# Differential score matmuls: the key's low part taken as 64-row products of both maps, and tiles of queries regrouped

## The reference

```python
p1 = causal_block_probs(q[:, start:end, :, 0], k[:, :end, :, 0], start, scale)
p2 = causal_block_probs(q[:, start:end, :, 1], k[:, :end, :, 1], start, scale)
p = (p1 - lam * p2).astype(v.dtype)
outs.append(jnp.einsum('bhqk,bkhd->bqhd', p, v[:, :end]))
```

## Time and profile before

| | |
|---|---|
| median of 3 runs | 1959.62 us |
| the profiled execution's own time | 1960.08 us |
| its span, first to last instruction | 1958.3 us |
| granted TensorE clock, mean over the span | 0.999 of full |
| TensorE matmuls: busy, count | 1946.1 us (99%), 9316 |
| TensorE weight loads: busy | 1630.9 us (83%) |
| DVE, ACT, POOL busy | 53%, 47%, 54% |
| one head of stage B, from one head's first score matmul to the next's | 38.12 us |

### The profile page before, as it was taken

One profiled execution on the slowest core, in us unless ns is written; L12 is line 12 of the kernel. 1 busy time (PEld: TensorE's weight loads), 2 busy tenths in 40 slices (PEclk: granted clock), 3 DMA queues, 4 the chain that ended last, 5 costly groups with the idle time before them and its releaser, 6 DMA issues.

```text
span 1958.3 us, 28641 instructions
## 1 busy us (share of the span) xinstructions
PE 1946.1 (99%) x9316; PEld 1630.9 (83%) x9316; DVE 1035.7 (53%) x1906; ACT 928.1 (47%) x1648; POOL 1066.7 (54%) x1418
## 2 busy tenths in 40 slices
PE   9999999999999999999999999999999999999998
PEld 7888888888888888888888888888888888888887
DVE  5555888887655333321154668888875543333111
ACT  6344666676544222233344456666674442222332
POOL 5655454444555555557765645345445555555674
PEclk9999999999999999999999999999999999999999
DMA  6332222224542322233343322222245332222232
GB/s 248 109 120 86 87 85 88 76 81 138 191 145 86 107 96 96 96 110 96 104 135 121 114 81 92 81 79 90 90 161 185 117 101 94 99 96 95 82 93 91
DMA packets 117938, 212.62 MB, mean 109 GB/s; under 512 B 14290, under 2 KB 31698, under 8 KB 117332
## 3 DMA queue, kind: packets, MB, share of 16 engines
q1 hardware_dynamic: 100944, 176.47, 27.3%
q10 hardware_dynamic: 16900, 34.92, 5.0%
HBM read 194.03 MB, written 17.31 MB: 108 GB/s over the span
## 4 chain that ended last, share of the span: by engine, by line
PE 99%; DMA 0%; DVE 0%; ACT 0%; issue 0%; SPq 0%
PE proj L599 24%; PE proj L601 24%; PE proj L600 24%; PE score L599 2%; PE score L600 2%; PE score L601 2%; PE flip L672 2%; PE score L654 2%; PE score L832 1%; PE score L834 1%; PE score L658 1%; PE score L657 1%; PE att L580 1%; PE att L581 1%; PE att L579 1%; PE score L846 1%
## 5 line engine op out<-in xcount | busy, mean ns | idle before, releaser
L556 POOL TENSOR_TENSOR w_lo<-raw,w_hi 128x256 fp32r<-128x256 f32 x1372 | 1061.6, 806 | 870.2 <-ACT w_hi L1126 870.0
L599 PE MATMUL proj<-h_hi,w_hi 128*128 128x512 f32 x1568 | 619.2, 395 | 0.0
L601 PE MATMUL proj<-h_hi,w_lo 128*128 128x512 f32 x1568 | 611.7, 390 | 0.0
L600 PE MATMUL proj<-h_lo,w_hi 128*128 128x512 f32 x1568 | 610.7, 389 | 0.0
L1126 ACT ACTIVATE w_hi<-raw 128x1024 fp32r<-128x1024 f32 x344 | 362.7, 1056 | 193.7 <-PE proj L601 55.5
L601 PEld LDWEIGHTS proj<-h_hi,w_lo 128*128 128x128 f32 x1568 | 294.3, 188 | 62.6
L599 PEld LDWEIGHTS proj<-h_hi,w_hi 128*128 128x128 f32 x1568 | 294.6, 188 | 58.4 <-issue 0.6
L600 PEld LDWEIGHTS proj<-h_lo,w_hi 128*128 128x128 f32 x1568 | 294.8, 188 | 58.2
L599 PE MATMUL proj<-hid_hi,w_hi 128*128 128x512 f32 x330 | 129.0, 391 | 0.0
L601 PE MATMUL proj<-hid_hi,w_lo 128*128 128x512 f32 x330 | 128.5, 389 | 0.0
L600 PE MATMUL proj<-hid_lo,w_hi 128*128 128x512 f32 x330 | 128.4, 389 | 0.0
(11 more groups left out here) (408 smaller groups left out, 3146.2 us busy)
## 6 DMA issues: line engine op xcount, KB each, us to landing
raw<-in_w_in SPq DMA_DIRECT2D x224, 256.0 KB, 2.8
raw<-in_w_gate_up SPq DMA_DIRECT2D x176, 256.0 KB, 2.8
raw<-in_w_down SPq DMA_DIRECT2D x96, 192.0 KB, 2.4
gate_in<-gate_scratch ACTq DMA_DIRECT2D x48, 256.0 KB, 4.2
gate_scratch<-gate_out ACTq DMA_DIRECT2D x46, 256.0 KB, 2.0
raw<-in_w_mem_kv SPq DMA_DIRECT2D x32, 256.0 KB, 2.8
raw<-in_w_o_diff SPq DMA_DIRECT2D x32, 256.0 KB, 2.8
raw<-in_w_out SPq DMA_DIRECT2D x32, 256.0 KB, 2.8
```

What stands on the lines that cost most here:

```text
L556: ins = g.tensor_tensor(w_lo[s][:, cols], raw[s % 2][:, cols], w_hi[s][:, cols].bitcast(F32), ALU.subtract)
L599: mm(o, hi[:, c:c + width], rh, start=start and k == 0, stop=False)
L600: mm(o, hi[:, c:c + width], rl, start=False, stop=False)
L601: ins = mm(o, lo[:, c:c + width], rh, start=False, stop=stop and k == n - 1)
```

## The change

- The key's low parts of both maps lie in one tile `k_lo`: map 1's in rows 0 to 63, map 2's in rows 64 to 127. The zero halves and the two memsets that wrote them are gone.
- The low matmuls take 64 rows instead of 128: map 1's rows 0 to 63 of the array, map 2's rows 64 to 127. They stand alternately in the program and write different banks. One pair would share a bank; there TensorE waits on a semaphore of its own (`lower_done`).
- A step no longer holds one map but both maps of half the query tiles: first the long step (t = 3 and t = 1, 512 and 256 columns), then the short step (t = 2 and t = 0, 384 and 128 columns). In each the four high matmuls come first and then the four low ones. Maxima, exponentials, inverse sums, scaling and the combination follow this grouping; the second map's long tiles go to a new buffer `p_c`, and map 1's scaling is in two parts, of which the second stands behind a weight split on ACT.
- The short step waits for 6 of the head's 12 exponentials instead of 8.
- The latent scores keep a function of their own without the branch for maps. `SPLIT` swaps outputs 10 and 6, since `p_c` lies over part of `outs_hi`, and ACT's wait for `att_read` in the last head stands earlier. In `last_head` the calls change as in `head`. Semaphore counts follow (`score_full` 8 a head instead of 9, `inv_ready` and `p_scaled` 2 instead of 1).

```diff
-SPLIT = (0, 1, 2, 3, 4, 5, 8, 9, 10, 6, 12, 13, 11, 14, 15, 7)
+SPLIT = (0, 1, 2, 3, 4, 5, 8, 9, 6, 10, 12, 13, 11, 14, 15, 7)
...
-        k1_lo, k2_lo = over_x("k1_lo_zero", 4), over_x("k2_zero_lo", 5)
+        k_lo = over_x("k1_lo_k2_lo", 4)
...
-                for k in ("m", "d1", "d2")}
-        lam_scale = here("lam_scale", [P, NT])
+                for k in ("m", "long", "short")}
+        lam_scale = {k: here(f"lam_scale_{k}", [P, NT]) for k in ("long", "short")}
...
+        p_c = at("p_c", 53 * KB, [P, 6 * P])
...
+        def map_tiles(part):
+
+            if part == "long":
+                return ((score[0][:, 0:512], 0, 3), (score[1][:, 0:512], 1, 3), (score[2][:, 0:256], 0, 1), (score[2][:, 256:512], 1, 1))
+            return ((score[0][:, 0:384], 0, 2), (score[0][:, 384:512], 0, 0), (score[1][:, 0:384], 1, 2), (score[1][:, 384:512], 1, 0))
+
+        def map_home(part, second, t):
+
+            if not second:
+                return p_b[:, q_off(t):q_off(t) + (t + 1) * P]
+            if part == "short":
+                return p_a[:, q_off(t):q_off(t) + (t + 1) * P]
+            return p_c[:, 0:512] if t == 3 else p_c[:, 512:768]
...
-            def causal_scores(l, h, n):
-
-
-                pe.wait_ge(exp_done.sem, exp_done.at(l, "B", h, 4 * n))
+            def map_scores(l, h, part):
+
+                pe.wait_ge(exp_done.sem, exp_done.at(l, "B", h, 4 if part == "long" else 6))
+                upper, lower = slice(0, 64), slice(64, P)
+                for n, (o, second, t) in enumerate(map_tiles(part)):
+                    q, k = ((q1, k1), (q2, k2))[second]
+                    opens = n != 3 if part == "long" else n % 2 == 0
+                    mm(o, q[:, t * P:(t + 1) * P], k[:, 0:(t + 1) * P], start=opens, stop=False)
+
+                def low(b, c, second, t, k0, width, stop):
+                    rows, q = (lower, q2) if second else (upper, q1)
+                    return mm(score[b][:, c:c + width], q[rows, t * P:(t + 1) * P], k_lo[rows, k0:k0 + width], start=False, stop=stop)
+                if part == "long":
+                    low(2, 256, 1, 1, 0, 256, False).then_inc(lower_done.sem, 1)
+                    low(0, 0, 0, 3, 0, 512, True).then_inc(score_full.sem, 1)
+                    low(1, 0, 1, 3, 0, 512, True).then_inc(score_full.sem, 1)
+                    pe.wait_ge(lower_done.sem, lower_done.at(l, "B", h, 1))
+                    low(2, 0, 0, 1, 0, 256, True).then_inc(score_full.sem, 1)
+                else:
+                    for t, c, last in ((2, 0, False), (0, 384, True)):
+                        for second in range(2):
+                            ins = low(second, c, second, t, 0, (t + 1) * P, last)
+                            if last:
+                                ins.then_inc(score_full.sem, 1)
+
+            def causal_scores(l, h):
+
+                pe.wait_ge(exp_done.sem, exp_done.at(l, "B", h))
                 for b, group in enumerate(((3,), (2, 0), (1,))):
                     for t in group:
                         o = score[b][:, 384 * (t == 0):384 * (t == 0) + (t + 1) * P]
                         cols = slice(t * P, (t + 1) * P)
-                        if n == 0:
-                            ins = mm(o, mqT[0:96, cols], mkT[0:96, 0:(t + 1) * P], start=t != 0, stop=t == group[-1])
-                        else:
-                            q, k, k_lo = ((q1, k1, k1_lo), (q2, k2, k2_lo))[n - 1]
-                            mm(o, q[:, cols], k[:, 0:(t + 1) * P], start=t != 0, stop=False)
-                            ins = mm(o, q[:, cols], k_lo[:, 0:(t + 1) * P], start=False, stop=t == group[-1])
+                        ins = mm(o, mqT[0:96, cols], mkT[0:96, 0:(t + 1) * P], start=t != 0, stop=t == group[-1])
                     ins.then_inc(score_full.sem, 1)
...
-                causal_scores(l, h, 1)
+                map_scores(l, h, "long")
                 causal_flip(l, h, 0, 0)
                 unit(l, "B", h, 1, 1, (ssq_read, ssq_read.at(l, "B", h)) if h else (v_copied, v_copied.at(l, "B", 0, 1)),
                      KD, h_rhs, w=w(1)).then_inc(slot_done.sem, 1)
                 causal_flip(l, h, 0, 1)
-                causal_scores(l, h, 2)
+                map_scores(l, h, "short")
                 unit(l, "B", h, 2, 0, (v_copied, v_copied.at(l, "B", n, 1)), KD, h_rhs, w=w(2)).then_inc(slot_done.sem, 1)
                 latent_attend(l, h)
...
+            def map_exps(l, h, part):
+
+                _, bias, total, _ = stat[part]
+                act.wait_ge(bias_ready.sem, bias_ready.at(l, "B", h, 2 if part == "long" else 3))
+                for c, (src, second, t) in enumerate(map_tiles(part)):
+                    sc.activation(map_home(part, second, t), src, ACT.Exp, bias=bias[:, c:c + 1], scale=DIFF_SCALE,
+                                  accum_out=total[:, c:c + 1]).then_inc(exp_done.sem, 1)
...
-            def scale_first(l, h):
-
-                act.wait_ge(inv_ready.sem, inv_ready.at(l, "B", h, 1))
-                for t in range(NT):
-                    s = p_b[:, q_off(t):q_off(t) + (t + 1) * P]
-                    ins = sc.activation(s, s, ACT.Copy, scale=stat["d1"][3][:, t:t + 1])
+            def scale_first(l, h, part):
+
+                act.wait_ge(inv_ready.sem, inv_ready.at(l, "B", h, 1 if part == "long" else 2))
+                for c, (_, second, t) in enumerate(map_tiles(part)):
+                    if not second:
+                        s = map_home(part, 0, t)
+                        ins = sc.activation(s, s, ACT.Copy, scale=stat[part][3][:, c:c + 1])
                 ins.then_inc(p_scaled.sem, 1)
...
-                exps(l, "B", h, 1, "d1", p_b, DIFF_SCALE)
+                map_exps(l, h, "long")
                 split_ahead(l, "B", h, 1, h)
                 causal_high(l, h, 0, 1)
-                scale_first(l, h)
+                scale_first(l, h, "long")
                 if h:
                     act.wait_ge(att_read.sem, att_read.at(l, "B", h))
                     outs_high(l, h - 1)
                 act.wait_ge(flip_full.sem, flip_full.at(l, "B", h, 4))
-                exps(l, "B", h, 2, "d2", p_a, DIFF_SCALE)
+                map_exps(l, h, "short")
                 split_ahead(l, "B", h, 2, h)
+                scale_first(l, h, "short")
                 query_high(l, n)
                 copy_gate(l, "B", h, 2, 0, 0)
...
                 att_mla(l, h)
+                act.wait_ge(att_read.sem, att_read.at(l, "B", h))
                 for k in SPLIT[6:9]:
                     outs_high(l, k)
...
+            def map_maxima(l, h, part):
+
+                top, bias, _, _ = stat[part]
+                full = 3 if part == "long" else 6
+                if part == "long":
+                    ve.wait_ge(score_full.sem, score_full.at(l, "B", h, full + 1))
+                    v.tensor_tensor(score[0][:, 384:512], score[0][:, 384:512], mask[:, 0, :], ALU.add)
+                    ve.wait_ge(score_full.sem, score_full.at(l, "B", h, full + 3))
+                    v.tensor_tensor(score[1][:, 384:512], score[1][:, 384:512], mask[:, 0, :], ALU.add)
+                    halves = score[2][:, :].rearrange("p (a n) -> p a n", a=2)
+                    chain(v.tensor_tensor(halves[:, :, 128:256], halves[:, :, 128:256], mask[:, :, :], ALU.add))
+                else:
+                    ve.wait_ge(score_full.sem, score_full.at(l, "B", h, full + 2))
+                    for b in range(2):
+                        s = score[b][:, 256:512]
+                        ins = v.tensor_tensor(s, s, mask[:, :, :].rearrange("p a n -> p (a n)"), ALU.add)
+                    chain(ins)
+                for c, (src, _, _) in enumerate(map_tiles(part)):
+                    ins = v.tensor_reduce(top[:, c:c + 1], src, AX.X, ALU.max)
+                chain(ins)
+                v.tensor_scalar(bias[:, :], top[:, :], -DIFF_SCALE, None, ALU.mult).then_inc(bias_ready.sem, 1)
...
-                invert(l, "B", h, 2, "d2")
-                chain(v.tensor_scalar(lam_scale[:, :], stat["d2"][3][:, :], gl[:, G_LAM:G_LAM + 1], None, ALU.mult))
-                ve.wait_ge(p_scaled.sem, p_scaled.at(l, "B", h, 1))
-                for t in range(NT):
-                    s = slice(q_off(t), q_off(t) + (t + 1) * P)
-                    ins = v.scalar_tensor_tensor(p_b[:, s], p_a[:, s], lam_scale[:, t:t + 1], p_b[:, s], ALU.mult, ALU.add)
+                for n, part in enumerate(("long", "short")):
+                    ve.wait_ge(inv_ready.sem, inv_ready.at(l, "B", h, n + 1))
+                    chain(v.tensor_scalar(lam_scale[part][:, :], stat[part][3][:, :], gl[:, G_LAM:G_LAM + 1], None, ALU.mult))
+                    ve.wait_ge(p_scaled.sem, p_scaled.at(l, "B", h, n + 1))
+                    for c, (_, second, t) in enumerate(map_tiles(part)):
+                        if second:
+                            first = map_home(part, 0, t)
```

(3 more changed lines are left out.)

## The result

The changed kernel takes 1963.52 us (median of 18 runs, 1962.87 to 1964.73), the kernel before 1959.75 (18 runs beside them, 1959.39 to 1960.29). The ratio is 1.0019, 95% interval 1.0012 to 1.0026: slower by 3.8 us, resolved, though just inside the 0.2% (3.9 us) that the prediction had taken as the least that can be told. The forecast was 1952.1, its range ended at 1963.0, and its sign was wrong. The median is 1.2 us from the first price of rival 1 (1962.3).

The account below looks back on a forecast made before the run. TensorE's own stream was taken as the bound: scores falling from 2.52 to 2.04 us a head, 0.47 taken as saved, 7.5 us over 16 heads, from 1960.08 to 1952.6, median 1952.1. Range 1949.0 to 1963.0.

Parts of the forecast that it names:

- rival 1: Changing between 128-row and 64-row matmuls empties the array, 0.16 us a change: 1962.3, or 1969.4 with loads exposed; chance 0.22.
- What bounds the kernel: TensorE, 99% busy, never waits for a softmax; only its own stream's start-to-start cost or a new wait moves the time.
- The order's gain: In both maps' scores, short matmuls no longer following each other save the 0.20 us a head lost to weight loads.
- The halves side by side: Low matmuls of both array halves overlap, with weight loads one at a time 0.11 us apart; chance 0.46.
- The change of rows: Going between 128-row and 64-row matmuls, four times a head; the forecast sum booked nothing for it.
- The wait for `lower_done`: In the long step, the fourth low matmul waits for the first one's results: some 0.05 us a head.
- DVE, ACT and new waits: Edits on DVE and ACT cost 0, within 0.3 us for a layer's last head; slack at unit 3 near 0.9 us.
- rival 3: A new TensorE wait at unit 3 or the transposes, each 0.3 us giving back 4.2 us: 1956.3; chance 0.04.

Follow-up runs that it names:

- x1_grouped_zeros: The changed kernel with zero halves and 128-row low matmuls back and no wait on lower_done: 1960.29 us, ratio 1.0002 to the kernel before.
- x5: The changed kernel with the short step's four low matmuls issued twice: 1968.3 us, ratio 1.0042 to the kernel before.
- x6: The changed grouping with zero halves, 128-row low matmuls and no lower_done wait, the short step's low matmuls issued twice: 1969.22 us, ratio 1.0047 to the kernel before.
- x3: The changed kernel without the low matmul of map 2's tile t = 1 and without the wait on lower_done: 1961.13 us, ratio 1.0006 to the kernel before.
- x2_64_rows_old_order: The kernel before with only its low matmuls narrowed to 64 rows, in the old order: 2006.47 us, ratio 1.0238.
- x11_one_window_final: The changed kernel reordered: a head's eight low matmuls in one 64-row stretch, weight and output splits moved behind copies TensorE needs: 1955.14 us, ratio 0.9976 to the kernel before.

## Why the prediction was wrong

Its forecast was a saving of 0.47 us a head, and the runs show a loss of 0.20. The steps, in its order:

- **What bounds the kernel**: right. TensorE's own stream decides, and the span moved by 16 times the change in the two stretches, to 0.2 us net.
- **The order's gain, 0.20 us a head**: failed. It is 0 (`x1_grouped_zeros`). I split a map's starts into slow and quick matmuls and took the quick ones as free to be had everywhere. The right reading adds the loads up: four 128-column matmuls need four loads of 0.11 us. The long step at 128 rows came out as counted (1.39 us, 1.40 in `x1_grouped_zeros`); the error is in the short step, where the 128-column matmuls now stand.
- **The halves side by side**: right, and better than forecast: loads of different halves start together instead of 0.11 us apart. A set of the short step costs 0.28 instead of 0.57 (`x5`, `x6`).
- **The change of rows, priced at 0**: failed, and this is the largest error. Rival 1 named it: emptying, 0.16 us a change, four times a head, or more with the load exposed. The runs show 0.28 us a stretch, thus 0.14 a change, 0.56 a head. That is over the 0.12 from which rival 1 was to decide. Its split was off: on the way in about 0.10 of emptying and 0.10 of exposed load, with a part of it covered. Emptying was over-priced (the low loads start at 231.36, before the last high results are out at 231.15 + 0.28 = 231.43), and the load was not priced in the first figure.
- **The wait for `lower_done`, 0.05 us a head**: failed. It costs 0.21. The moment was nearly right: the fourth matmul starts 0.44 us after the first, and I had 0.38. What I left out is 0.06 from the result to the start of the load and that the load lies bare (0.10). With 0.10 for leaving the 64 rows, which belongs to the step above and which `x3` has too, the 0.50 for the end became 0.75.
- **DVE, ACT and new waits**: right. There is no new wait in the heads, and rival 3 is out; the one at `sum_lo` lies outside them, and I had not looked there.

In one line, a head against before: two stretches save 0.29 in the short step and about 0.30 in the long one (`x3` is 0.02 us a head under `x1`, after paying 0.28), cost 0.28 each, and the wait adds 0.21. That is -0.59 + 0.56 + 0.21 = +0.18, measured +0.20. Against the forecast the errors are 0.20 for the order, 0.56 for the changes of rows and 0.16 for the wait, and some 0.26 the other way for halves that overlap better: 0.66 of the 0.67 us between -0.47 and +0.20. So the two stretches alone would have ended about even, and it is the wait that made the kernel slower than before. That the median comes so near to rival 1's 1962.3 is partly luck: that figure has no wait of this size in it, it books the order gain that isn't there, and it prices the changes at 0.64 instead of 0.56.

The Trainium skill, TensorEngine Tiling (Array Packing), section Key Properties, says that changing the mode drains TensorE, and I gave it 0.22. The trace agrees in that the next load stands 0.10 us behind the last columns; it does not wait for the last results. The argument from the earlier trace rows against it, that 96 rows go in and out freely, concerns another case: going to 96 rows had no price here, going to 64 did, and the 96-row matmuls are also plain float32. The Trainium skill's other rule, TensorE: Matmul & The Clock Gate, Part 3, that matmuls in different row groups start about 4 ns apart, is borne out with float32r: pairs that start together are 0 to 7 ns apart in the changed kernel's trace, most of them 3. Which of the two rules wins depends here on how much is saved in a stretch.

Open: whether the spacing to GpSimd's split makes `sum_lo` 0.57 us longer, and why `x3` gives back 3.5 us in its score sum and only 2.4 in the median. `sum_lo` is long in both kernels, so it is not that. Laid side by side, the two traces show 0.12 us more ahead of the attention in `x3`, 0.11 more at `sum_lo`, and some 0.04 us a head more in the projection units, in steps of 0.01 us and with no wait listed. What makes these was not found. The long step whole and without its wait was not run, since its two 256-column tiles share a bank.

## What to carry to other kernels

Using the array's other half saves what it halves, and costs a price for each stretch of narrow matmuls, here 0.28 us (0.36 around each of the single ones of `x2_64_rows_old_order`), somewhat more than the 0.23 us of a 512-column matmul; gather narrow matmuls into one long stretch, and leave them at 128 rows with zeros where less than that is saved. Measure a stretch from the instruction ahead of it to the second one behind it, as part of its price stands there. And put other matmuls between one that signals and one that waits for it on TensorE, or the wait lays bare a weight load as well: with two between it cost 0.21 us, with six nothing, and numbers between were not tried.

## What was not expected of the hardware

- Weight loads of two different row halves run at the same time (both at 231.36), while loads of one region are 0.11 us apart.
- A wait of TensorE on its own result cost 0.21 us though the result came only 0.05 us later than the matmul could have started without it; the weight load behind the wait does not go ahead.
- Matmuls of different halves need not start in program order: in all 16 heads of `x11_one_window_final` the last low matmul of the program starts 0.05 us before the one ahead of it, which is in the other half.
- Behind a 64-row stretch the second matmul starts late (0.34 us after the first, 0.23 elsewhere; 0.28 behind a 128-row one of 128 columns in `x1_grouped_zeros` and `x6_zeros_short_lows_twice`).
